# Down weights of the first block's experts loaded as four adjacent rows per partition, gated rows turned by every fourth column

## What is computed

```python
def expert_choice_ffn(h, w_router, w_gate, w_up, w_down):
    cap = CAPACITY_FACTOR * S // N_EXPERTS            # 64 tokens an expert
    aff = jax.nn.softmax(logits, axis=-1)
    gate, idx = lax.top_k(aff.transpose(0, 2, 1), cap)
    xe = jax.vmap(lambda hb, ib: hb[ib])(h, idx)
    hid = jax.nn.silu(jnp.einsum('becd,edf->becf', xe, w_gate)) * jnp.einsum('becd,edf->becf', xe, w_up)
    ye = jnp.einsum('becf,efd->becd', hid, w_down) * gate[..., None].astype(h.dtype)
    return ... # scattered back to the tokens and added
```

## Time and profile before

| | |
|---|---|
| median of 3 runs | 2679.06 us (2676.0 to 2679.06) |
| profiled execution | 2672.59 us |
| its span, first to last instruction | 2670.9 us |
| TensorE busy | 2480.8 us, 93% of the span |
| VectorE, ScalarE, GpSimd busy | 1123.1, 851.2, 307.4 us |
| moved by DMA | 646.27 MB, mean 242 GB/s |
| mean granted TensorE clock | 0.963 of full speed |

### The profile page before, as it was taken

The page is one execution under the profiler, slowest core; times in us unless marked ns, Lnnn a source line. Parts: engine busy times, 40 slices in busy tenths (PEclk is TensorE's granted clock), DMA queues, the critical chain, the costliest instruction groups (busy, mean ns, idle before and its releaser), DMA issues. The chain is left out here.

```text
span 2670.9 us, 31960 instructions
## 1 busy us (share of the span) xinstructions
PE 2480.8 (93%) x12976; PEld 1479.0 (55%) x12976; DVE 1123.1 (42%) x1736; ACT 851.2 (32%) x1161; POOL 307.4 (12%) x122
## 2 busy tenths in 40 slices
PE   5989799999997989799999996999999999989998
PEld 4734533333335735433333334887788787766665
DVE  4985312222224885312222225565322112456765
ACT  4235111111114245111111115566432344245553
POOL 0002000000000011000000002001433452200000
PEclk8999899999998989899999997999999999989999
DMA  9702579999999502489999993322233331149995
GB/s 344 265 1 80 204 303 409 410 410 410 410 408 336 204 0 95 190 337 409 410 410 410 409 394 95 91 83 80 79 103 102 102 120 64 48 166 375 360 352 205
DMA packets 276277, 646.27 MB, mean 242 GB/s; under 512 B 12098, under 2 KB 110656, under 8 KB 276160
## 3 DMA queue, kind: packets, MB, share of 16 engines
q1 hardware_dynamic: 269038, 631.78, 63.0%
q0 software_dynamic: 2592, 7.87, 0.8%
q10 hardware_dynamic: 4528, 4.98, 0.6%
HBM read 639.88 MB, written 6.29 MB: 242 GB/s over the span
## 5 line engine op out<-in xcount | busy, mean ns | idle before, releaser
L759 PE MATMUL ps<-ring,scr 128*64 128x512 f32 x1952 | 428.3, 596 | 1.4 <-DMA ring<-in_w_up 1.4
L759 PEld LDWEIGHTS ps<-ring,scr 128*64 128x64 f32 x1952 | 139.1, 138 | 280.9 <-issue 275.4
L1432 POOL TENSOR_TENSOR raw_r<-raw,w_high 128x2048 fp32r<-128x2048 f32 (+1 forms) x44 | 192.4, 4379 | 464.9 <-ACT w_high L1686 464.9
L781 PE MATMUL ps<-ring,scr 128*64 128x512 f32 x1024 | 230.2, 603 | 1.4 <-ACT scr L953 1.4
L1448 PE MATMUL ps<-x_high,w_high 128*128 128x512 f32 x480 | 195.0, 406 | 10.7 <-DVE y L2067 5.7
L1450 PE MATMUL ps<-x_high,raw_r 128*128 128x512 f32 x480 | 191.2, 398 | 0.0
L1449 PE MATMUL ps<-xT_r,w_high 128*128 128x512 f32 x480 | 190.5, 397 | 0.0
L1009 DVE SCALAR_TENSOR_TENSOR one_hot_T<-h_tok,convw,one_hot_T 128x512 f32<-128x512 f32 x240 | 170.4, 763 | 1.7
L469 POOL TENSOR_TENSOR one_hot_T_r<-hy,one_hot_T_r 128x1024 fp32r<-128x1024 f32 x16 | 38.5, 2409 | 1121.5 <-ACT one_hot_T_r L965 1121.5
L1218 DVE TENSOR_TENSOR scr<-scr,ps 128x512 f32<-128x512 f32 x32 | 22.0, 688 | 318.7 <-PE ps L759 318.7
L2558 DVE TENSOR_TENSOR ring_r<-ring,ring_high 128x2048 fp32r<-128x2048 f32 x56 | 127.7, 2288 | 63.5 <-ACT ring_high L2436 63.4
(11 more groups left out here) (528 smaller groups left out, 4398.8 us busy)
## 6 DMA issues: line engine op xcount, KB each, us to landing
ring<-in_w_down SPq DMA_DIRECT2D x64, 2048.0 KB, 15.2
ring<-in_w_up SPq DMA_DIRECT2D x62, 2048.0 KB, 18.3
ring<-in_w_gate SPq DMA_DIRECT2D x60, 2048.0 KB, 14.9
ring<-in_w_up SPq DMA_DIRECT2D x56, 1024.0 KB, 7.6
ring<-in_w_ada SPq DMA_DIRECT2D x22, 2048.0 KB, 12.5
ring<-in_w_down SPq DMA_DIRECT2D x28, 1024.0 KB, 7.2
raw<-in_w_in SPq DMA_DIRECT2D x23, 1024.0 KB, 5.1
ring<-in_w_in SPq DMA_DIRECT2D x16, 512.0 KB, 10.4
```

Source lines behind the costliest of these rows:

```text
L759: mm = pe.matmul(ps[CAP * half:CAP * (half + 1), 1 + j // 2, :], x_e[:, at_x:at_x + CAP], weights[:, k, half * HALF:(half + 1) * HALF], st ...
L781: mm = pe.matmul(ps[CAP * half:CAP * (half + 1), 4, :], hidT[:, at_f:at_f + CAP], weights[:, k, half * HALF:(half + 1) * HALF], start=(j = ...
L1432: pool.tensor_tensor(dst, src, high.bitcast(F32), ALU.subtract).then_inc(w_ready, 1)
```

## The change

```diff
@@ layer @@
-    hidT = sg
+    hidT, hid_rows = sg, hid.rearrange("p (n b) -> p b n", b=4)
@@ load(e, j) @@
                 name, k = ("w_gate", "w_up", "w_down")[j // 2], 4 * (j % 2)
-                w = A[name][bass.ds(l, 1), bass.ds(e, 1)].rearrange("a e (k p) n -> p (a e k) n", p=P)
+                w = A[name][bass.ds(l, 1), bass.ds(e, 1), k * P:(k + 4) * P]
+                w = w.rearrange("a e (p k) n -> p (a e k) n", p=P) if j >= 4 else w.rearrange("a e (k p) n -> p (a e k) n", p=P)
                 place, landed, _ = expert_chunk(e, j)
-                sp.dma_start(place, w[:, k:k + 4]).then_inc(landed, 16)
+                sp.dma_start(place, w).then_inc(landed, 16)
@@ expert(e, last, scattered) @@
                 for b in range(4):
-                    mm = pe.transpose(ps[:, 3, b * P:(b + 1) * P], hid[:, b * P:(b + 1) * P], ident)
+                    mm = pe.transpose(ps[:, 3, b * P:(b + 1) * P], hid_rows[:, b, :], ident)
```

## The result

The changed kernel took 2683.4 us in the median of 20 runs (2676.85 to 2694.99), the kernel before 2678.88 us in the 20 runs beside it. The ratio is 1.0025, with a 95% interval from 1.0015 to 1.0035: **6.7 us slower, from 4.0 to 9.4**. I had forecast +0.2 us and 2679. The time lies in the range given, but the change made the kernel slower, at about the bound of what can be told from no change, and I had said that it would not.

The account below looks back on a forecast made before the run. TensorE was taken to bound the kernel by a hair, with loads just behind. Loads -1.8 us and transposes +2.0 us summed to +0.2 us, so 2679 us on the median, with a range from 2671 to 2694 us.

Parts of the forecast that it names:

- The bound: Expert stages: TensorE is the limit by a hair, with weight loads falling behind by 2.0 us a pair of experts.
- the waits: TensorE's waits for the late fourth chunk of expert 14, one in each layer, together 1.8 us, forecast to vanish.
- The loads: Down-chunk loads in expert stages: 16 KB runs at 613 ns save 0.22 us a chunk, -1.8 us in all.
- the late down chunks: Down-weight chunks issued late in an expert stage: forecast to land after some 17 us and not 21.7.
- The rival of slower runs: Down-chunk loads: 16 KB runs from 654 ns on make the kernel over 5.4 us slower, far end 2820 us; chance 0.07.
- that of transfers cut into 4 KB: Down-chunk loads: DMA hardware may cut runs into 4 KB pieces, the 1.8 us stay, 2681 us; chance 0.14.
- The transposes: Four an expert, reading columns at a step of 16 bytes: 0.06 us more an expert, +2.0 us in all.
- the halved rate: Transposes' weight loads: a 16-byte step halves the reading rate, 2 ns more for each of three, 57 for the first.
- The rival of dear reading: Transposes' weight loads: strided reading of 151 ns or more makes the kernel slower, 2687 to 2694 us; chance 0.15.
- The sum: Whole kernel: -1.8 us from loads and +2.0 from transposes give +0.2 us, 2679 us.
- the signs that I named: Profile checks: 244462 packets, down chunks after about 17 us, no expert 14 wait, pair period 59.4 to 59.6 us, loads near 190 ns.
- The rival of the faster side: Expert-stage load waits: timed runs wait up to 6.5 us more than the profiled one, giving 2673 us; chance 0.14.

Follow-up runs that it names:

- second run: Only the 16 KB runs of the down chunks, transposes reading adjacent columns as before, against the kernel before the change: 2673.93 us, ratio 0.9989 (0.9973 to 1.0006).

## Why the prediction was right or wrong

**The bound** was right. TensorE sets the pace and the loads stand just behind it: their better rate gave only the waits (second run), and the added ns of the transposes came out in full.

**The loads**: estimated 613 ns a run of 16 KB, and so it is; forecast 17 us for the late down chunks, 16.5 measured; -1.8 us, and both waits are gone. The rival of slower runs and that of transfers cut into 4 KB are out. Nothing here was mis-sized, and with the loads alone, without the step, it is 16.6 us.

**The transposes**: "I take the halved rate", +2.0 us. A load shows 209 ns, 69 more, where I had it near 190. From start to start it is 120 ns (the 1.44 us of twelve more) where I had 110: so three of the four cost 11 ns more each and not 2, and what is left for the first, 0.062 us, is near my 57 ns. Together 0.095 us an expert and not 0.063, 3.0 us. The term was a third too small, by what I took for hidden under a product. The rival of dear reading, from 151 ns of reading on, is not what happened: 57 + 69 = 126 ns.

**The sum** is the step that failed: "-1.8 + 2.0 = +0.2 us" holds stream and waits only. The terms as measured give +1.2 us. TensorE's clock had no term and no rival, though the mean granted clock of 0.963 says that 198 us of the profiled execution were at half clock, and its timeline had a fall of 1.7 us in each expert stage. The change brought 13 to 15 us more of it, an estimated 4 to 7 us: half-clock time 213.8 us (2.6) in the change, 214.6 (3.2) with the step alone, 200.1 (5.0) with the loads alone, against 200.0 (1.7) before. None of the signs that I named could have shown this: packets, late down chunks, waits and the period of a pair all came out as forecast. That the time lies in the range is luck, since the range reached that far for a dear stride, which didn't come. Over all 28 runs of the change the mean is 2684.4 us and over 98 of the kernel before 2677.8, 6.6 us apart.

**The rival of the faster side**, that the timed runs wait more for loads than the profiled one, is out: with the loads alone the time fell by 2.8 us in the median, not by 8. The 6.5 us between the median and the profiled execution are scatter of the runs, which goes in part with their clock: the correlation of time and half-clock time is 0.68 over 98 runs of the kernel before and 0.83 over the 20 of the change.

What stays open is how a stepped weight load raises the half-clock time, and how much of the rise is the step and how much the longer pair. The falls stand where the stretch of small products gives way to the down products, and in rows they come 61.4 us apart. Why four stepped transposes there go with more half-clock time and sixteen don't, these runs don't tell.

## What to carry to other kernels

A weight load that reads with a step has its cost mostly hidden under the product before it, yet on a bound TensorE it cost 3 us of stream and an estimated 4 to 7 us in clock. Put the step on an engine with room: the same permutation on VectorE cost 0.37 us an expert and nothing that the time shows. Larger runs for a queue that is only just behind the bound engine took away here the 1.8 us of waits that the trace names; a gain beyond that isn't shown.

When a TensorE-bound kernel moves by more than its stream does, work out the time at half clock from each run's mean clock before looking elsewhere, and compare means over many runs, since one profile shows one drawing of it.

## What I had not expected of the hardware

- A float32 weight load of a transpose (128 x 128) shows 140 ns with adjacent columns, 209 at steps of 8 and of 16 bytes, 191 at 32 bytes.
- DMA runs of 16 KB take 613 ns where four of 4 KB take 656 in the packet records and 640 by the rate; the rate in a full queue rose from 410 to 415 GB/s with a third of the bytes in such runs.
- Falls of the granted clock to 0.50 for 3.4 us, 1.7 us each, come in rows 61.4 us apart. In one profile each, pairs of 59.84 us had five in a row with stepped transposes and 16 KB loads, and pairs of 59.85 us none with neither.
- Work added to the bound engine can be nearly free: two plain transposes more an expert, 7.0 us in all, made the kernel 2 us slower in the median (interval -1.3 to +4.6 us).
